# A front stage with its units' chunks in another order, and sixteen subtractions moved from VectorE to GpSimd

## The reference, cut to what matters

```python
xn = rms_norm(x, norm1)
proj = xn @ w_in                              # hyena x0,x1,v | q | k | v: 1536 + 512 + 128 + 128 columns
y_hy = hyena_mixer(proj[..., :1536], ...)     # short_conv of width 3, then x0 * (filter conv (x1 * v)) by FFT at 2L
y_at = window_gqa(q, k, v, ...)               # |q-k| <= 128, 8 heads on 2 key heads
mixed = concat([rms_norm(y_hy, hy_gain), rms_norm(y_at, at_gain)])
h = x + mixed @ w_out
gate, up = split(rms_norm(h, norm2) @ w_gate_up)   # 2 x 2816 columns
return h + (silu(gate) * up) @ w_down
```

## Time and profile before

| | us |
|---|---|
| median of 3 runs | 2722.68 (2720.36 to 2727.37) |
| the profiled execution | 2724.04 |
| its span | 2722.3 |
| PE busy in the span | 2619.3 |
| granted TensorE clock, mean | 0.984 |

### The profile page before, as it was taken

One profiled execution on the slowest core, in us unless ns is written; L12 is line 12 of the kernel. 1 busy time (PEld: TensorE's weight loads), 2 busy tenths in 40 slices (PEclk: granted clock), 3 DMA queues, 4 the chain that ended last, 5 costly groups with the idle time before them and its releaser, 6 DMA issues.

```text
span 2722.3 us, 39455 instructions
## 1 busy us (share of the span) xinstructions
PE 2619.3 (96%) x13881; PEld 2394.6 (88%) x13881; DVE 2106.0 (77%) x2518; ACT 1372.8 (50%) x2375; POOL 1230.2 (45%) x1182
## 2 busy tenths in 40 slices
PE   8999999999898999999999999899999989999998
PEld 6888989888797888878999999899999989999997
DVE  6765664678448777867888888988888888888887
ACT  5564544477448787764343434443434443443432
POOL 1655211112112454465687764455554444444443
PEclk9999999999998999999999999999999999999999
DMA  7688967899996454455444443543333355333332
GB/s 232 194 281 233 318 208 222 278 287 277 249 223 181 128 146 126 127 163 156 131 139 140 138 119 121 185 139 113 113 112 102 93 182 159 91 92 89 90 90 89
DMA packets 470044, 446.33 MB, mean 164 GB/s; under 512 B 54670, under 2 KB 377358, under 8 KB 469559
## 3 DMA queue, kind: packets, MB, share of 16 engines
q1 hardware_dynamic: 441960, 372.22, 47.4%
q0 software_dynamic: 27888, 71.58, 8.4%
HBM read 329.90 MB, written 113.79 MB: 163 GB/s over the span
## 4 chain that ended last, share of the span: by engine, by line
PE 84%; DVE 7%; DMA 4%; issue 2%; SPq 2%; ACT 1%; POOL 0%; DVEq 0%; ACTq 0%; POOLq 0%
PE ff_banks L85 17%; PE ff_banks L86 17%; PE ff_banks L87 17%; PE pr_acc L85 4%; PE pr_acc L86 4%; PE pr_acc L87 4%; PE am_mix L85 2%; PE am_mix L87 2%; PE am_mix L86 2%; PE pr_gen L85 2%; PE am_turn L2359 2%; PE pr_gen L87 1%; PE pr_gen L86 1%; DMA sp_k<-k_dram 1%; PE am_score L2346 1%
## 5 line engine op out<-in xcount | busy, mean ns | idle before, releaser
L3494 DVE TENSOR_TENSOR ff_h<-ff_h,ff_banks 128x1536 f32<-128x1536 f32 x231 | 402.9, 1744 | 6.2 <-PE ff_banks L87 5.4
L3330 ACT COPY ff_r<-ff_banks 128x384 f32<-128x384 f32 x198 | 94.9, 479 | 593.2 <-PE ff_banks L87 593.1
L3477 DVE TENSOR_TENSOR ff_dlo<-ff_dlo_raw,ff_dhi 128x512 fp32r<-128x512 f32 x231 | 212.8, 921 | 173.4 <-ACT ff_dhi L3360 173.1
L85 PE MATMUL ff_banks<-ff_xhi,ff_ghi 128*128 128x384 f32 x924 | 313.5, 339 | 13.8 <-DVE ff_silu L3454 8.1
L85 PE MATMUL pr_acc<-pr_xhi,pr_whi 128*128 128x386 f32 (+1 forms) x864 | 305.2, 353 | 12.7 <-DVE pr_xlo L1682 7.7
L87 PE MATMUL ff_banks<-ff_xhi,ff_glo 128*128 128x384 f32 x924 | 311.7, 337 | 0.0
L85 PE MATMUL ff_banks<-ff_xhi,ff_uhi 128*128 128x384 f32 x924 | 310.8, 336 | 0.7 <-ACT ff_r L3330 0.6
L86 PE MATMUL ff_banks<-ff_xlo,ff_ghi 128*128 128x384 f32 x924 | 311.2, 337 | 0.0
L86 PE MATMUL ff_banks<-ff_xlo,ff_uhi 128*128 128x384 f32 x924 | 310.6, 336 | 0.0
L87 PE MATMUL ff_banks<-ff_xhi,ff_ulo 128*128 128x384 f32 x924 | 310.0, 335 | 0.0
L3178 POOL TENSOR_TENSOR ff_act<-ff_act,ff_silu 128x384 f32<-128x384 f32 x99 | 116.6, 1177 | 419.6 <-issue 234.1
(11 more groups left out here) (353 smaller groups left out, 6692.2 us busy)
## 6 DMA issues: line engine op xcount, KB each, us to landing
ff_glo_raw<-w_gate_up SPq DMA_DIRECT2D x132, 256.0 KB, 3.0
ff_ulo_raw<-w_gate_up SPq DMA_DIRECT2D x132, 256.0 KB, 3.0
ff_dlo_raw<-dsum_dram SPq DMA_DIRECT2D x132, 256.0 KB, 2.7
pr_raw<-w_in SPq DMA_DIRECT2D x108, 256.0 KB, 5.8
ff_dlo_raw<-w_down SPq DMA_DIRECT2D x99, 256.0 KB, 2.6
sp_k<-k_dram SPq DMA_DIRECT2D x64, 256.0 KB, 5.6
pr_xs<-x SPq DMA_DIRECT2D x18, 512.0 KB, 5.7
xkeep_dram<-pr_xs SPq DMA_DIRECT2D x18, 512.0 KB, 4.5
```

What stands on the lines that cost most here:

```text
L85: pe.matmul(out, still[0], moving[0], start=start, stop=False, skip_group_check=goes_on)
L3330: act.copy(kept[n][:], bank(X)).then_inc(copied, 1)
L3477: dve.tensor_tensor(dlo[d_slot(n)][:], din[d_slot(n)][:], dhi[d_slot(n)][:].bitcast(F32), ALU.subtract).then_inc(d_low, 1)
L3494: dve.tensor_tensor(to, to, lowered_all(k), ALU.add).then_inc(added, 1)
```

## The change

It has two parts, which share no tile.

**The order.** `abreast` names the outer pairs of units of a round: its first two, and (but in the last round) its last two. In these the four events go chunk by chunk: unit 0 chunk 0, unit 1 chunk 0, unit 0 chunk 1, unit 1 chunk 1. `event`, `chunks`, `unit_of`, `u_number` and `hyena_number` follow; the bank of `acc` is now the event's parity, and not the chunk. Turns 0, 1 and 2 of the next round start one event earlier (two events are still to come, `unit_done` at `2 * first_unit - 2`), turns 3 to 6 spread over the first two events of the round, since chunk 1 is needed from the third on. Weights are issued at the first event of each unit as before; in the outer pairs that is one event earlier for the second unit, and its first use too.

**The subtractions.** `octet_low` leaves DVE and stands in POOL's `product_step`, ahead of `store_z(j - 4)`. Sixteen operations of 128x1024.

```diff
+    def abreast(r, i):
+        return i < 2 or r < ROUNDS - 1 and i >= units_of(r) - 2
+    def place_of(r, i, c):
+        return i // 2 * 4 + 2 * c + i % 2 if abreast(r, i) else 2 * i + c
     def event(r, i, c):
-        return 2 * (first_unit(r) + i) + c
+        return 2 * first_unit(r) + place_of(r, i, c)
...
             if r:
                 lift(r, 3)
                 seam(r)
-                evict(r - 1, units_of(r - 1) - 1, 1)
+                evict(r - 1, *chunks(r - 1)[-1])
+                yield
+                norm(GT * r + GT - 1)
                 yield
...
-            turn(r, 3)
...
-            for i in range(units_of(r)):
+            for at, (i, c) in enumerate(order):
                 n = first_unit(r) + i
-                if n + 1 < UN:
+                if n + 1 < UN and c == (abreast(r, i) and i % 2):
                     weights(n + 1)
-                now[0] = event(r, i, 0)
+                now[0] = event(r, i, c)
                 u_turn(now[0])
-                first_half(r, i, 0)
-                if i == 0:
-                    turn(r, 4)
+                first_half(r, i, c)
+                if at == 0:
+                    turn(r, 3 if r else 4)
...
+                if at == 1:
+                    turn(r, 5 if r else 6)
...
+                if at == end - 1 and goes_on:
                     turn(r + 1, 1)
                 yield
...
+                second_half(r, i, c)
+                if at == end and goes_on:
+                    break
...
+                evict(r, i, c)
+                if at == 0:
+                    turn(r, 4 if r else 5)
+                if at == 1 and r and peeks(r):
+                    turn(r, 6)
+                if at == end - 2 and goes_on:
+                    turn(r + 1, 0)
+                if at == end - 1 and goes_on:
                     turn(r + 1, 2)
+                yield
...
             if rd and j < 3:
-                act.wait_ge(unit_done, 2 * first_unit(rd) - 1)
+                act.wait_ge(unit_done, 2 * first_unit(rd) - 2)
...
+            if j < 2:
+                pool.wait_ge(product, products(j + 1))
+                pool.tensor_tensor(yf[:, j, 0, :], pa[:, 0, :], pb[:, 1, :], ALU.subtract).then_inc(y_summed, 1)
+                pool.tensor_tensor(yf[:, j, 1, :], pa[:, 1, :], pb[:, 0, :], ALU.add).then_inc(y_summed, 1)
+            if j < NOCT:
+                octet_low(j)
             if j >= 4:
                 store_z(j - 4)
...
+        def octet_low(t):
+            pool.wait_ge(ha_high, t + 1)
+            pool.tensor_tensor(alo[:, t % 3], ha[:, t % 3], ahi[:, t % 2].bitcast(F32), ALU.subtract).then_inc(ha_low, 1)
...
-        def octet_low(t):
-            dve.wait_ge(ha_high, t + 1)
-            dve.tensor_tensor(alo[:, t % 3], ha[:, t % 3], ahi[:, t % 2].bitcast(F32), ALU.subtract).then_inc(ha_low, 1)
```

More of the change, by code:

```diff
@@ L155, in hyena_number @@
     def hyena_number(r, i, c):
-        return event(r, i, c) if r < NG else 2 * NU + 2 * CT * (r - NG) + 2 * x0_tile(i) + c
+        if r < NG:
+            return event(r, i, c)
+        return 2 * NU + 2 * CT * (r - NG) + place_of(r, i, c) - (0 if i < 2 else 12)
     def other_number(r, i, c):
@@ L212, in unit_of @@
             if e < 2 * first_unit(r + 1):
-                return r, e // 2 - first_unit(r), e % 2
+                return r, *chunks(r)[e - 2 * first_unit(r)]
     def u_number(e):
-        return 2 * (e // 4) + e % 4 - 2 if 2 <= e % 4 and e < 16 * NG else None
+        if e >= 16 * NG:
+            return None
+        r, i, c = unit_of(e)
+        return 8 * r + i // 2 * 2 + c if i % 2 else None
     def v_event(e):
@@ L261, in course @@
         norm(3)
+        turn(0, 2)
         for r in range(ROUNDS):
-            end = units_of(r) - 1
+            order = chunks(r)
+            end, goes_on = len(order) - 1, r < ROUNDS - 1
             if r:
@@ L302, in course @@
+                if c and 1 <= i <= 4 and goes_on:
                     norm(GT * r + GT + i)
[L303 removed]
+                if at == end - 1 and goes_on:
                     turn(r + 1, 1)
                 yield
[L306 to L313 removed]
+                second_half(r, i, c)
@@ L1165, in half_chunk @@
             for k in ks:
-                last = triple(pe, acc[:, c, 0:o.stop - o.start], (whi[:, n % 2, k, :], wlo[:, n % 2, k, :]),
+                last = triple(pe, acc[:, event(rd, i, c) % 2, 0:o.stop - o.start], (whi[:, n % 2, k, :], wlo[:, n % 2, k, :]),
                               (xhi[:, k, o], xlo[:, k, o]), k == 0, k == KT - 1)
@@ L1441, in evict @@
             act.wait_ge(unit_done, event(rd, i, c) + 1)
+            a = event(rd, i, c) % 2
             if is_hyena(rd, i):
@@ L1474, in evict @@
             for a0, a1, o in kept(rd, c):
-                last = act.copy(dst[:, a0:a1], acc[:, c, 1 + a0 + o:1 + a1 + o])
+                last = act.copy(dst[:, a0:a1], acc[:, a, 1 + a0 + o:1 + a1 + o])
             last.then_inc(other_out, 1)
```

35 lines of the change are left out of this document (16 added, 19 removed).

## The result

The changed kernel took 2727.14 us in the median of 20 runs (2720.68 to 2733.02), the kernel before 2722.82 us in 20 runs beside it (2713.74 to 2729.67). The ratio is 1.0015 with a 95% interval of 1.0008 to 1.0022: 4 us slower. That is inside the 0.3% that I called no change, which I gave 0.45; but the forecast was 2718 us, 4.5 us faster, and the change went the other way.

The account below looks back on a forecast made before the run. PE, busy 2619.3 of 2722.3 us, was taken as the bound. Round starts with clock -15.5 and subtractions +11 gave -4.5 from 2724.0, so 2719.5; with the median 1.4 lower, 2718 us, range 2700 to 2732.

Parts of the forecast that it names:

- The starts of the rounds: PE's standstills where rounds two to six start would mostly go, as tiles gain an event: 9.5 us won.
- Second round: Start of round two: PE's 3.10 us wait for bank space, behind the copy `ust` on ACT, would go; gain 2.9.
- Third round: Start of round three: `xlo` was last ready, and turns 0 to 2 begin an event sooner; gain 2.5.
- Fourth round: Start of round four: only two `xlo` pieces stay ahead of the first eviction, one `wlo` may remain; gain 3.1.
- Fifth round: Start of round five: gain 3.0, less 2 because loads issued ahead delay the prompt's `ur_us`; gain 1.0.
- Sixth round: Start of round six: 2.77 us go, but PE comes sooner to the 5.5 us wait for `ir_zlo`; gain 0.
- The clock: Windows at the starts of rounds two to five: half of 12.2 us of missing PE clock comes back, 6 us.
- The subtractions: Product loop: `alo` on POOL delays DVE's `ylo`, 18.5 us over fourteen turns, 7.5 absorbed in `sp_k` waits; cost 11 us.
- The third: Rival, chance 0.15: turns' waits only move, the third event waiting where the second did; +6 us, 2729 us.
- part one: The new order's effect at the round starts, standstills and clock together: -15.5 us, between -24 and -5.
- The first: Rival, chance 0.20: GpSimd's work costs nothing, as `ylo` or `yf` gets ahead of `alo`; -21 us, 2702 us.
- The second: Rival, chance 0.15: GpSimd's operation takes longer than 2.37 us, delaying `ylo`; with 3.4 us +9.5, 2732 us.

Follow-up runs that it names:

- The order alone: The changed kernel with all `octet_low` subtractions back on DVE, so only the new order against the kernel before: 2726.98 us, ratio 1.0010.
- turns early again: The new order, all subtractions on DVE, turns 3 to 6 moved earlier again, at or near their old places: 2716.25 us, ratio 0.9977 to the kernel before.
- the subtractions alone: The kernel before, in its old order, with only `octet_low` moved to POOL as in the change: 2729.60 us, ratio 1.0026.
- the stores first: The kernel before, with fourteen octets' subtractions on POOL behind its stores and DVE's sum, the first two on DVE: 2728.26 us, ratio 1.0022.

## Why the prediction was wrong

**The starts of the rounds, -9.5 us forecast.** This is the step that failed. I counted the events that each row tile's turn gained and not what it was put behind. "The new order gives each tile an event more" is true for PE's need of turns 4 to 6, but their instructions went behind others in DVE's and ACT's order by as much or more; and of turn 3 it is not even true in the third and the sixth round, where PE's first event waits for its two `MEMSET`s. The order alone, forecast at -15.5 us with its clock, cost 2.7 (0 to 5.4 by its interval); with its turns early again it won 6.3.
- Second round, -2.9 forecast: the old wait for `ust` went as said, and a wait of 3.4 us for the low part of the filter's `fi_h` came in its place. Nothing was won there (-1.1 us at the round before's second last event, -1.7 at this round's third).
- Third round, -2.5 forecast: 2.5 us lost (-0.7 to 1.8). I had taken `xlo` for the last thing ready; it was the `MEMSET`s of turn 3 (290.61), while the `xlo` beside them ended after PE's start. Turn 3 now stood behind a norm, a copy and `wlo`; with it moved back the standstill halved. I had these rows ahead of me in the order of the fourth round and priced `wlo` only.
- Fourth round, -3.1 forecast: 4.2 won (1.9 to -2.3), the one round where it came out, and in part by luck. Before, PE's start at 391.24 followed not the four pieces, which end at 389.9, but an eviction and then turn 6's two small pieces (391.03). The 2.47 us that stayed are turn 6 at the third event, and not the one `wlo` that I allowed for; with the turns early again 7.2 us were won here.
- Fifth round, -1.0 forecast: 7.3 lost (-2.3 to 5.1). `ur_us` landed when it had landed before (ACT took it at 512.41 us, 512.36), so PE's 2.3 us were waited away, as my 2 us said, though not by a later load. The rest I had not seen: turn 5's `xlo`, and behind it turn 6's two small pieces (537.57), for which PE waits 5.44 us, now stand behind the whole second product step on DVE (`pa`, `pb`, `ylo`), where before that step, of which the earlier trace rows are a part, came behind turns 4 to 6. Another 2.0 us went to a new wait of PE for the first product's `pb`.
- Sixth round, 0 forecast: right in kind. The wait for `ir_zlo` takes up what comes before it, gains and losses alike.

**The clock, -6 us forecast.** It hung on the standstills and fell with them; of the four windows only the fourth round's rose, from 0.86 to 0.93, and the third round's fell from 0.93 to 0.86.

**The subtractions, +11 us forecast.** Right in mechanism and place, and its size within the bounds: 7 us in the subtractions alone. `alo` took 2.41 us for 2.37; from `pb`'s start to `yf`'s it is now 4.53 us, and was 3.42, so 1.11 later for 1.32 forecast. The waits for `sp_k` fell by 12.2 us in the subtractions alone, but those for `crossed` at the same instruction rose to 10.6 from

```profile
DVE sp_pb L1872 <- ACT sp_crossed L1605: 6.2, 9, 0.7
```

so 7.8 us were absorbed, where I took 7.5. Fourteen turns of 1.11 less 7.8 are 7.7, near the 7 measured (4 to 10 by its interval): the term was too large by the 0.2 us a turn. Of the changed kernel's own loss in the loop, 5 us in both traces, this is not shown, as the order alone loses 5.2 and 3.6 there without any subtraction on POOL.

**The rivals.** The third, that the turns' waits only move, had 0.15 and was 2729 us: it is what happened, with 2727, and with its sign, third events that wait 2 us or more. That its number is so near is luck: it was priced from saturated queues and still gave part one 5 us, while the reason was the order of instructions on DVE, and part one lost 2.7. The first, that POOL's work costs nothing, named "`ylo` gets ahead" as its way; the runs show that this is not enough. The second, that POOL takes longer, is excluded by the 2.36 to 2.42 us of its fourteen turns in the changed kernel's trace. What the prediction calls the second rival, in its sentence on the order of issue, is this first one.

## What to carry to other kernels

A piece of work that is given a later due time is not thereby earlier than it: list what stands ahead of it on its own engine at its new place, and price all of that against the due time. Read the due time from the waits of the engine that uses it: a semaphore that counts several pieces holds that engine until the last of them, needed or not. Where an engine's subtractions go to GpSimd, the question is which of VectorE's instructions run in the 2.4 us after the start; the place behind the last instruction that would be shut out, ahead of ones that read PSUM, was worth 6.5 us here for the same work. And a store that the same engine issues must not be put behind such work, if a buffer waits for it (ACT waited 3.15 us here).

## What the runs showed of the hardware

That a copy within SBUF on VectorE with one input, of 128x384, is held up by a GpSimd subtraction as much as a two-input operation (0.36 us became 1.78 to 2.11 in nine turns of the stores first) was not in my theory, which named two inputs alone. The Trainium skill ("SBUF — State Buffer", section "Who interferes with whom") says it: a `copy` can run in a mode that uses both pairs of ports and then contends with GpSimd. These runs agree, and with its rule that the order of issue decides: `ylo` ahead of `alo` took 1.23 us, behind it 2.58. Beside such a GpSimd subtraction `oc` (0.61 us) and the products `pa` (1.28 us for two), which take one of their two tensors from PSUM, lost nothing; by the same section an instruction with at most one input in SBUF, outside those modes, does not contend, and the traces agree. `oc` also takes `gq`, one value per partition, from SBUF, of which the section does not speak.
